# Steps change places in a one-core kernel of two transformer blocks, and eleven MLP blocks multiply the normalised stream

## What is computed

```python
h = (_rms(x) * (1.0 + scale_m) + shift_m).astype(dt)
proj = jnp.einsum('bsd,de->bse', h, w_in[l])
...
x = x + gate_m * jnp.einsum('bse,ed->bsd', mixed, w_out[l])
h = (_rms(x) * (1.0 + scale_f) + shift_f).astype(dt)
u = jnp.square(jax.nn.relu(jnp.einsum('bsd,df->bsf', h, w_mlp_in[l])))
x = x + gate_f * jnp.einsum('bsf,fd->bsd', u, w_mlp_out[l])
```

## Time and profile before

| | |
|---|---|
| median of 3 runs | 780.11 us (779.64 to 782.59) |
| profiled execution, whole / span in the profile | 780.57 / 778.8 us |
| mean granted TensorE clock | 0.998 of full speed |
| TensorE busy | 757.2 us, 97% |
| VectorE busy | 602.0 us, 77% |
| ScalarE busy | 379.8 us, 49% |
| GpSimd busy | 27.5 us, 4% |
| loaded from memory | 154.07 MB, 199 GB/s over the span |

### The profile page before, as it was taken

How to read it: one execution, slowest core, us unless ns; L and a number is a source line. 1 busy time by engine, 2 the same in 40 slices (tenths; PEclk the granted TensorE clock), 3 DMA queues, 4 the chain that set the end, 5 groups by cost and what they waited for, 6 DMA issues and landing times.

```text
span 778.8 us, 15072 instructions
## 1 busy us (share of the span) xinstructions
PE 757.2 (97%) x6382; PEld 744.0 (96%) x6382; DVE 602.0 (77%) x917; ACT 379.8 (49%) x516; POOL 27.5 (4%) x22
## 2 busy tenths in 40 slices
PE   8999999999999999999999999999998999999998
PEld 8999998999989999999999999999998999999998
DVE  5666898978896688988898688968877778876573
ACT  6657345653676443434335457356455443344431
POOL 0000000002010000000000000201100000000000
PEclk9999999999999999999999999999999999999999
DMA  9844273342653459988887335555344367764511
GB/s 338 309 157 146 84 259 109 109 162 108 256 179 109 163 215 385 345 307 317 289 323 257 109 117 213 214 177 203 109 167 158 128 252 274 266 217 166 214 56 55
DMA packets 24115, 156.10 MB, mean 200 GB/s; under 512 B 3568, under 2 KB 3696, under 8 KB 6000
## 3 DMA queue, kind: packets, MB, share of 16 engines
q1 hardware_dynamic: 24048, 155.13, 55.2%
HBM read 154.07 MB, written 1.05 MB: 199 GB/s over the span
## 4 chain that ended last, share of the span: by engine, by line
PE 75%; DVE 13%; ACT 6%; issue 4%; DMA 1%; POOL 0%; SPq 0%; DVEq 0%; ACTq 0%
PE bank L764 14%; PE bank L766 14%; PE bank L765 14%; PE bank L837 7%; PE bank L840 7%; PE bank L839 7%; DVE sb_lo L1693 4%; ACT sb_hi L1363 3%; PE bank L1229 2%; PE bank L772 2%; PE bank L774 1%; PE bank L775 1%; PE bank L1196 1%; PE bank L1206 1%; DMA sb_raw<-in_stream 1%
## 5 line engine op out<-in xcount | busy, mean ns | idle before, releaser
L1693 DVE TENSOR_TENSOR sb_lo<-sb_raw,sb_hi 128x2048 fp32r<-128x2048 f32 (+1 forms) x116 | 261.9, 2260 | 96.7 <-ACT sb_hi L1363 96.2
L1363 ACT CAST sb_hi<-sb_raw 128x2048 fp32r<-128x2048 f32 (+1 forms) x116 | 217.0, 1877 | 46.6 <-PE bank L840 38.3
L764 PE MATMUL bank<-sb_u_hi,sb_hi 128*128 128x256 f32 (+2 forms) x576 | 164.9, 286 | 0.0
L766 PE MATMUL bank<-sb_u_hi,sb_lo 128*128 128x256 f32 (+2 forms) x576 | 161.8, 281 | 0.0
L765 PE MATMUL bank<-sb_u_lo,sb_hi 128*128 128x256 f32 (+2 forms) x576 | 161.8, 281 | 0.0
L837 PE MATMUL bank<-sb_hid_hi,sb_hi 128*128 128x256 f32 x432 | 120.2, 278 | 0.0
L840 PE MATMUL bank<-sb_hid_hi,sb_lo 128*128 128x256 f32 x432 | 120.2, 278 | 0.0
L839 PE MATMUL bank<-sb_hid_lo,sb_hi 128*128 128x256 f32 x432 | 120.1, 278 | 0.0
L764 PEld LDWEIGHTS bank<-sb_u_hi,sb_hi 128*128 128x128 f32 (+2 forms) x576 | 107.8, 187 | 3.2 <-issue 2.2
L766 PEld LDWEIGHTS bank<-sb_u_hi,sb_lo 128*128 128x128 f32 (+2 forms) x576 | 109.2, 190 | 0.2
L765 PEld LDWEIGHTS bank<-sb_u_lo,sb_hi 128*128 128x128 f32 (+2 forms) x576 | 108.1, 188 | 0.4
(11 more groups left out here) (365 smaller groups left out, 1424.5 us busy)
## 6 DMA issues: line engine op xcount, KB each, us to landing
sb_raw<-in_stream SPq DMA_DIRECT2D x140, 1024.0 KB, 5.1
sb_raw<-in_stream SPq DMA_DIRECT2D x4, 256.0 KB, 5.9
sb_raw<-in_stream SPq DMA_DIRECT2D x2, 512.0 KB, 8.3
sb_mem_t<-in_mem SPq DMA_DIRECT2D x1, 1024.0 KB, 4.9
out<-sb_h SPq DMA_DIRECT2D x4, 256.0 KB, 2.9
sb_const<-in_constants SPq DMA_DIRECT2D x1, 830.0 KB, 10.9
sb_h<-in_x SPq DMA_DIRECT2D x1, 572.0 KB, 3.6
sb_h<-in_x SPq DMA_DIRECT2D x1, 512.0 KB, 6.2
```

The source lines that it names most:

```text
L764: nc.tensor.matmul(out, a_hi, b_hi, start=(i == 0), stop=False)
L766: last = nc.tensor.matmul(out, a_lo, b_hi, start=False, stop=(i == n - 1))
L1363: nc.scalar.copy(place(hi, s)[:, 0:n], x[:, 0:n]).then_inc(sem("hi_ready"), 1)
L1693: tt(place(lo, s)[:, 0:n], x[:, 0:n], f32(place(hi, s)[:, 0:n]), ALU.subtract) \
```

## The change

Two kinds of edits. In `plan()`, steps change places: norms (`ssq_cols`, `rstd`, `diag`, `rstd_row`), the pieces of the top-k, `merge_sum` and `merged_lo`, `turn_mixed`, `ret_scores`, `log_f`, and the rounding and residues of weight blocks, most of which go behind the residual adds or sums of squares that they stood ahead of, with the rounding put in earlier on its own. And the `mlp_in` blocks from `RAW_MLP = 5` on, the sixth to the sixteenth, multiply the normalised stream in `u_hi`, `u_lo` with 256 columns, made by eight `u_norm` steps of norm 6, four behind `mlp_in 2` and four behind `mlp_in 3`. For these blocks both halves go to one bank, ScalarE takes the ReLU straight from it in one instruction of 512 elements, and VectorE has no part in the evacuation.

```diff
@@ -204,13 +204,14 @@
     def shifted(n, s):
 
         for k in range(KD):
-            if 2 <= k < 6:
-                add("ssq_cols", n, k - 2)
-            if k == 5:
+            if 2 <= k < 4:
+                add("ssq_cols", n, 2 * k - 4)
+                add("ssq_cols", n, 2 * k - 3)
+            if k == 3:
+                add("rstd", n)
                 split(s + 2)
-                add("rstd", n)
                 add("diag", n)
-            if k == 7:
+            if k == 6:
                 add("rstd_row", n)
             add("raw", n, k)
         for k in range(KD):
@@ -267,21 +268,21 @@
     block("gate", 3, between=[("cmp_product", 0, 1), ("cmp_hidden", 0), ("topk", 0, 0)])
     steps([("cmp_product", 1, 0), ("topk", 0, 1), ("turn_qk", 2)])
     block("gate", 4, between=[("cmp_product", 1, 1), ("cmp_hidden", 1), ("cmp_hid",), ("topk", 0, 2)])
-    steps([("index", 1), ("turn_qk", 3), ("topk", 0, 3)])
+    steps([("index", 1), ("turn_qk", 3)])
     block("gate", 5, between=[("cmp_kv",)])
-    steps([("scores", 4), ("scores", 5), ("topk", 1, 0), ("turn_o", 0)])
+    steps([("scores", 4), ("scores", 5), ("topk", 0, 3), ("turn_o", 0)])
     block("gate", 6, ahead=False, between=[("cmp_scores",), ("rounds", "gate", 8)])
     steps([("turn_p", 4), ("turn_p", 5), ("scores", 6), ("scores", 7)])
-    block("gate", 7, ahead=False, between=[("pv", 4), ("pv", 5), ("turn_cmp_p",), ("split", "gate", 8), ("topk", 1, 1), ("turn_qk", 6)])
-    steps([("turn_p", 6), ("turn_p", 7), ("scores", 8), ("scores", 9), ("topk", 1, 2), ("split", "gate", 9)])
+    block("gate", 7, ahead=False, between=[("pv", 4), ("pv", 5), ("turn_cmp_p",), ("split", "gate", 8), ("topk", 1, 0), ("turn_qk", 6)])
+    steps([("turn_p", 6), ("turn_p", 7), ("scores", 8), ("scores", 9), ("topk", 1, 1), ("split", "gate", 9)])
     block("gate", 8, ahead=False, evac_now=False, between=[("cmp_pv",), ("o_group", 1)])
     steps([("rounds", "gate", 10), ("pv", 6), ("pv", 7), ("turn_p", 8), ("turn_p", 9), ("scores", 10), ("scores", 11)])
     evac(where["gate", 8])
-    steps([("split", "gate", 10), ("topk", 1, 3)])
+    steps([("split", "gate", 10), ("topk", 1, 2)])
     block("gate", 9, ahead=False, evac_now=False, between=[("pv", 8), ("pv", 9)])
     steps([("rounds", "gate", 11), ("turn_p", 10), ("turn_p", 11), ("scores", 0), ("scores", 1)])
     evac(where["gate", 9])
-    split(where["gate", 11])
+    steps([("split", "gate", 11), ("topk", 1, 3)])
     block("gate", 10, ahead=False, evac_now=False, between=[("pv", 10), ("pv", 11)])
     steps([("rounds", "up", 0), ("turn_p", 0), ("turn_p", 1), ("scores", 2), ("scores", 3)])
     evac(where["gate", 10])
@@ -292,7 +293,7 @@
     split(where["up", 2])
     block("up", 0, ahead=False, between=[("merge", 0, 0), ("merge", 0, 1), ("pv", 2), ("pv", 3), ("turn_o", 2),
                                          ("merge", 0, 2), ("split", "up", 1), ("merge", 0, 3)])
-    block("up", 2, ahead=False, between=[("merge", 1, 0), ("merge", 1, 1), ("turn_o", 1)])
+    block("up", 2, ahead=False, between=[("merge", 1, 0), ("merge", 1, 1), ("rounds", "out", 0), ("turn_o", 1)])
     split(where["out", 0])
     add("merge", 1, 2), add("merge", 1, 3)
     block("up", 1, ahead=False)
@@ -301,9 +302,9 @@
     add("merge", 2, 2), add("merge", 2, 3), add("merge_sum", 1)
     split(where["out", 1])
     add("merged_lo", 1)
-    for c in (2, 3):
-        add("merge_sum", c)
-        add("merged_lo", c)
+    rounds(where["out", 2])
+    add("merge_sum", 2), add("merge_sum", 3)
+    add("merged_lo", 2), add("merged_lo", 3)
     block("out", 0)
     block("out", 1)
     for c in range(4):
@@ -318,7 +319,8 @@
     split(where["mem_v",])
     add("rstd_row", 1)
     evac(where["mem_k",])
-    block("mem_q", ahead=False, between=[("ssq_cols", 2), ("rstd", 2), ("split", "mem_o")])
+    block("mem_q", ahead=False, between=[("split", "mem_o")])
+    add("ssq_cols", 2), add("rstd", 2)
     rounds(where["ffn_in", 0])
     add("mem_v", 0)
     for u in range(12, 16):
@@ -364,17 +366,19 @@
             add("mod", 0)
         if i == 9:
             add("shift", 0)
-    block("ffn_out", 10)
+    block("ffn_out", 10, ahead=False)
+    rounds(where["proj2", 1])
     table = parts["second"] = []
     residual(2, 5)
+    split(where["proj2", 1])
     shifted(5, where["proj2", 0])
     after = {0: [], 1: [("rope2", 0)], 2: [("diag", 4)], 3: [("rstd_row", 4), ("rope2", 1)],
              4: [("turn_ret", 0), ("turn_ret", 1)],
              5: [("turn_ret", 2), ("turn_ret", 3), ("forget",), ("final_norm",)],
-             6: [("fox_square", 0), ("log_f",)], 7: [("forget_sum",), ("fox_norm", 0)],
+             6: [("log_f",), ("fox_square", 0)], 7: [("forget_sum",), ("fox_norm", 0)],
              8: [("fox_square", 1), ("ret_scores", 0), ("ret_scores", 1)],
              9: [("fox_norm", 1)],
-             10: [("ret_pv", 0), ("ret_pv", 1), ("ret_scores", 2), ("ret_scores", 3)],
+             10: [("ret_scores", 2), ("ret_scores", 3), ("ret_pv", 0), ("ret_pv", 1)],
              11: [("ret_pv", 2), ("ret_pv", 3), ("scores", 16), ("scores", 17), ("o_group", 8)],
              12: [("turn_p", 16), ("turn_p", 17), ("scores", 18), ("scores", 19), ("mix", 0, 0)]}
     inside = {10: [("turn_fox", i) for i in range(4)], 11: [("turn_fox", i) for i in range(4, 8)]}
@@ -392,19 +396,23 @@
            ("mix_gate", 0, 0), ("ada_bias", 12, 20), ("mod", 1)])
     block("proj2", 15, between=[("pv", 20), ("pv", 21), ("mix_gate", 0, 1), ("mix", 1, 0)])
     steps([("turn_p", 22), ("turn_p", 23), ("mix_scale", 1, 0)])
-    block("proj2", 16, ahead=False, between=[("pv", 22), ("pv", 23), ("turn_mixed", 2), ("turn_mixed", 3)])
-    steps([("mix_tanh", 1), ("mix", 1, 1), ("split", "out2", 3), ("mix_gate", 1, 0)])
+    block("proj2", 16, ahead=False, between=[("pv", 22), ("pv", 23), ("turn_mixed", 2), ("turn_mixed", 3),
+                                                 ("rounds", "out2", 3)])
+    steps([("mix_tanh", 1), ("mix", 1, 1), ("split", "out2", 3), ("mix_gate", 1, 0), ("rounds", "out2", 0)])
     block("out2", 2, ahead=False)
     steps([("mix_scale", 1, 1), ("mix_gate", 1, 1), ("split", "out2", 0)])
-    block("out2", 3)
-    steps([("turn_mixed", 0), ("turn_mixed", 1), ("shift", 1)])
+    block("out2", 3, ahead=False, between=[("rounds", "out2", 1), ("turn_mixed", 0), ("turn_mixed", 1)])
+    steps([("split", "out2", 1), ("shift", 1)])
     block("out2", 0, ahead=False)
     block("out2", 1, ahead=False)
+    split(where["mlp_in", 0])
+    rounds(where["mlp_in", 1])
+    residual(3, 6)
     split(where["mlp_in", 1])
-    residual(3, 6)
     table = parts["mlp"] = []
-    block("mlp_in", 0, evac_now=False)
+    block("mlp_in", 0, evac_now=False, ahead=False)
     sum_squares(6)
+    split(where["mlp_in", 2])
     block("mlp_in", 1, evac_now=False, between=[("ssq_cols", 6), ("rstd", 6), ("diag", 6)])
     add("rstd_row", 6)
     for i in range(2):
@@ -414,6 +422,9 @@
         block("mlp_in", i)
         block("mlp_out", i - 2)
         add("hidden", where["mlp_in", i])
+        if i < 4:
+            for k in range(4 * i - 8, 4 * i - 4):
+                add("u_norm", 6, k)
         if 3 <= i < 7:
             more_ada()
         if i == 8:
@@ -445,6 +456,7 @@
 MEM_Q, FFN_0, PROJ2_0, MLP_0 = (BLOCK_AT[b] for b in (("mem_q",), ("ffn_in", 0), ("proj2", 0), ("mlp_in", 0)))
 IDLE = {("block", 0): 16, ("mem_o", 0): 3}
 OUT2_BANK = (4, 0, 1, 2)
+RAW_MLP = 5
 MLP_BANK = ((5, 4), (0, 1), (5, 4), (6, 7))
 O_BANK = {0: 2, 1: 2, 3: 3, 4: 2, 2: 3, 5: 3, 10: 0, 6: 2, 7: 3, 8: 2, 9: 3}
 TURNS = [("QA", 0), ("KA", 2), ("QC", 4), ("KSW", 6), ("QI", 8), ("KIB", 10), ("QB", 12)]
@@ -906,6 +918,15 @@
 
             def mlp_in(s, j, cut):
 
+                if j >= RAW_MLP:
+                    if j == RAW_MLP:
+                        pe.wait_ge(sem("u6_lo"), KD)
+                    key = ("block", s)
+                    last = by_feature(s, key, MLP_BANK[2 + j % 2][0], u_hi, u_lo, None, cut)
+                    if cut != 0:
+                        fill(last, key)
+                        used_at[s] = (key,)
+                    return
                 w_hi, w_lo = weights(s)
                 keys = [("mlp", j, m) for m in range(2)]
                 if j == 0:
@@ -1383,6 +1404,10 @@
                 if kind == "mlp_in":
                     if j >= 2:
                         act.wait_ge(sem("hidden_ready"), 22 + j - 1)
+                    if j >= RAW_MLP:
+                        ps = wait_filled(act, key)
+                        free(nc.scalar.activation(act_out[:, j % 2, :], ps[:, :], ACT.Relu), key)
+                        return
                     for m in range(2):
                         wait_evacuated(act, ("mlp", j, m))
                         x = slice(m * T, m * T + T)
@@ -1716,7 +1741,7 @@
                         last = ts(vm[:, t, :], ps[:, t * T:t * T + T], rstd[:, 1, t:t + 1], None, ALU.mult)
                     free(last, ("block", s))
                     return
```

(16 more changed lines are left out.)

## The result

The changed kernel took 769.83 us in the median (768.44 to 774.74, 4 runs) against 781.35 us (779.64 to 784.50, 4 runs) for the kernel before on the same chip: a ratio of 0.9855, 95% interval 0.9825 to 0.9886. It is faster, and the time is inside the range (758.5 to 770.0), but at its upper end, 5.8 us above the forecast of 764.0. The profiled execution took 770.07 us against 780.57, a gain of 10.5 where the sum said 16.1.

The account below looks back on a forecast made before the run. TensorE, busy 97% of the span, was taken as the bound: its work plus its waits. Terms summing to 16.1 us off the profiled 780.57 gave 764.5; the median lies 0.46 lower, so 764.0, range 758.5 to 770.0.

Parts of the forecast that it names:

- Top-k, merges, memory norms, forget gate, out2, norm 6: TensorE waits removed by reordering: top-k 0.75, merges with memory norms 3.1, forget gate with retention 1.4, out2 1.3, norm 6 2.8 us.
- VectorE is the real bound of the short stages: Rival: waits in the reordered stages come back later, half of 9.9 us lost, 769.0 us; chance 0.12.
- The clock at 120 us: Behind the `cmp_scores` wait: the half-clock stretch from 120.2 to 123.6 us goes, gaining 1.6 us.
- Second block's first norm: First raw product starts 0.5 us sooner, wait for the first normalised part falls from 1.2 to 0.4: gain 1.3 us.
- The first rival: The clock falls all the same, at 120 us or behind another wait, costing 1.6: 765.6 us; chance 0.22.
- MLP, narrow blocks: Sixth to 16th `mlp_in` blocks at 256 columns take 5.45 instead of 5.80 us each: gain 3.85 us.
- the second form of that rival: All MLP blocks from the sixth on run at the feed-forward pace, 5.65 us: 768.8 us; chance 0.15 for both forms.
- MLP, the cover: Added MLP work overruns VectorE by 2.7 us but costs nothing, weight blocks being split a block and more ahead.
- The feed-forward part's pace: Rival: 31 feed-forward blocks go at 5.45 instead of 5.65 us, 6.2 us less, 757.8 us; chance 0.05.

Follow-up runs that it names:

- e2: The kernel before with the MLP part of the change alone, order of everything else as before; 779.52 us, ratio 1.0029.
- e9: The kernel before with four one-column matmuls added ahead of `ffn_out 0`; 777.42 us, ratio 0.9959.
- e8: The changed kernel without normalising steps, MLP on the wide stream, sixth to 16th block 256 columns for seven feature blocks of eight; 766.45 us, ratio 0.9815.
- e14: The changed kernel itself, run again beside e15; ratio 0.9847 to the kernel before, profiled execution 775.45 us.
- e11: The changed kernel with four one-column matmuls ahead of `ffn_out 0`, two normalising steps an iteration, `ada` at iterations 6 to 9, narrow blocks from the eighth; ratio 0.974.
- e15: The program of e11 run once more, beside e14; ratio 0.9742 to the kernel before.
- e7: The changed kernel with its four `ada` steps at iterations 6 to 9 instead of 3 to 6; 772.17 us, ratio 0.9893.

## Where the prediction was right, and where it failed

- **Top-k, merges, memory norms, forget gate, out2, norm 6:** foreseen 0.75 + 3.1 + 1.4 + 1.3 + 2.8 = 9.35, measured 0.9 + 3.4 + 1.8 + 4.6 = 10.7. The mechanism was the one named: a residue that ran ahead of a short step went behind it, and the waits did not come back elsewhere; "VectorE is the real bound of the short stages" is refuted for these stages. At norm 2 GpSimd's power step, now behind the residue and not beside it, took 0.70 us in place of 2.67, as argued. The 1.4 us more are of the kind that I left out (a wait costs a little more than the list says) by letting them cancel against the slower pace.
- **The clock at 120 us:** 1.6 foreseen and measured, but the term was a draw. Three profiles have the old order there and a wait of about 1.5 us from start to start (the kernel before, `e2`, `e9`); the clock fell in one. Nor does it take more than such a wait, as the prediction had it: in `e9` the clock also fell behind the wait of 1.8 us at norm 6, behind which it held in the kernel before and in `e2`.
- **Second block's first norm, the second step that failed:** "which I reckon leaves 0.4 us of the wait: gain 0.5 + 0.8 = 1.3". With the clock up it is 0.6 + 0.45 = 1.1: the wait for the normalised part went down to 0.2, but one of 0.5 for the diagonal came, because the residue placed behind `rstd` makes GpSimd's step 2.0 us longer, which the prediction had read at norm 2 and left at nothing here. The larger loss, 2.4 us, is a half clock of 6.75 us. The first rival has a fall at 120 us "or behind another wait", at 1.6; this one came with no wait ahead of it, in 7 of 13 profiles, so the sum has no term for it.
- **MLP, narrow blocks:** 11 x 0.35 = 3.85 came to the hundredth in this execution. That is a draw too: in 5 of 14 profiles all of the MLP's narrow part goes at 117.8 ns, as the second form of that rival had it, and the term is lost. The width alone is 0.20 of the 0.35 (`e8`).
- **MLP, the cover: the step that failed.** "7.7 more does overrun one pair by 2.7 us, but the weight blocks are split a block and more ahead". The lead was 4.2 us, not a block (5.45 us) and more, and the first bunch of steps left 0.3 of it. I took it from the plan and never read it in the trace, and counted VectorE's sum over a pair of blocks when the steps stand in two bunches. ScalarE's eight steps, costed at nothing, hold the roundings: 1.2 us of the wait. The wait came to 2.8 us from start to start and 1.4 of half clock behind it. "Without that cover it would cost the 2.7 us" has the right size by luck: 1.0 of it is `ada`, which stood there before, and 1.2 ScalarE, which that sum does not hold.
- **Sum:** 16.1 - 2.6 (norm) - 4.2 (MLP) + 1.4 (elsewhere) = 10.7; the profiled executions lie 10.5 apart.
- **The feed-forward part's pace** did not change with the edit, as the rival had it at 0.05; but its price, 6.2 us, is what the faster pace is worth there (6.1 from `ffn_out 0` on).

## What to carry to other kernels

Before a step of an in-order engine is costed at nothing, read the lead in the trace: when the prepared block is ready and when it is wanted, and put the added steps between in the order of the queue, on every engine that the prepared block passes through. Spread such work over the iterations instead of bunching it. An effect that was read in one place (here a residue beside GpSimd's power step) is to be looked for wherever the new order makes the same neighbours. Where one form of matmul shows two paces at a full clock, find the instruction at which the pace turns, try a burst of short ones at the head of the next block, and judge a change of 1% only against profiles that show which pace each stage had.

## What the runs showed of the hardware

- The same matmul of 256 columns with its weight load goes at 113.3 or 117.8 ns from start to start at the 2.4 GHz level, steadily for over 1,000 instructions (1,500 in the feed-forward part of the changed kernel), and bursts of short float32 matmuls switch it, as a float32 matmul of 256 columns did in 4 of 18 profiles. The Trainium skill (TensorE: Matmul & The Clock Gate, Back-to-back issue gap) says that in a stream of weight loads and matmuls both set the spacing and gives one spacing for each width, for an isolated matmul N/2.4 + 2.5 ns; the estimate by it is 109.2 for 256 columns. These traces do not agree with a single figure: both paces lie above it, and the width is the same.
- Executions of one program differ by up to 12 us (763.06 to 775.45 for the changed kernel), and where two were profiled (the changed kernel and `e14`, `e11` and `e15`), most of the difference is the MLP at the one pace or the other, 5 us, and beside it in `e15` a half clock of 2.4. In the feed-forward part the pace would be worth 6; 17 of the 18 profiles go into it at 117.8.
- The granted clock fell to the 1.2 GHz level at the end of a wait of 2.6 us at the first narrow block in 6 of 7 profiles that have it, behind waits of 1.6 and 2.0 us in the MLP (`e7`, `e2`) in neither, behind a wait of 1.8 us at norm 6 in 1 of 3 (`e9`), and, with no wait ahead of it, in or soon behind the second group of short matmuls at 434 us in 7 of 13.
- GpSimd's power of 128x2 numbers took 0.69 to 0.71 us, and 2.67 to 2.68 us where VectorE started a residue (2.29 us) beside it. This holds in all 18 profiles: at norm 2 in the three with the old order there, at norm 5 in the 14 that have a residue right behind `rstd`, and nowhere else.
